# Delta rule's block inverses: the coupling products of both directions, head by head in turn

## The chip, the cores and the metric

The kernel runs on one core of one Trainium2 chip. The metric is the time of one execution on the device, in microseconds (us); the lower, the better. TensorE multiplies matrices, VectorE and ScalarE read its results from PSUM and write them to SBUF, GpSimd does elementwise work from SBUF to SBUF, and the sync engine issues most of the loads.

## The reference

The model is a two-layer backbone over 512 latent tokens and 256 context tokens, 1024 features wide, with feed-forward blocks and adaptive norms around one mixer in each layer. The first layer's mixer has neighbourhood attention beside a gated delta rule, which runs over the tokens in both directions, with four heads of 128 features. Per chunk of tokens and head the delta rule solves a triangular system:

```python
kb = k * beta[..., None]
L = jnp.where(strict, jnp.einsum('bnhcd,bnhsd->bnhcs', kb, k) * decay, 0.0)
A = L + jnp.eye(C, dtype=jnp.float32)
rhs = jnp.concatenate([v * beta[..., None], kb * jnp.exp(g)[..., None]], -1)
sol = lax.linalg.triangular_solve(A, rhs, left_side=True, lower=True, unit_diagonal=True)
u, w = sol[..., :dv], sol[..., dv:]
```

After that a scan over the chunks carries the state S:

```python
v_new = u_i - jnp.einsum('bhcd,bhde->bhce', w_i, S)
o = jnp.einsum('bhcd,bhde->bhce', q_i, S) + jnp.einsum('bhcs,bhse->bhce', qk_i, v_new)
S = S * gl[..., None, None] + jnp.einsum('bhcd,bhce->bhde', k_i, v_new)
```

All arithmetic is float32. Context tokens come first in each direction, and the state they leave starts the latent tokens.

## The kernel before, in words

The whole model is one program for one core, written out engine by engine. `schedule()` makes one list of items, each a piece of TensorE work with its place in PSUM. Every engine walks this list in the same order and picks its share of each item. TensorE executes its queue in list order; at the end of an item it raises the semaphore `product_done` by one, so that a reader of item i waits for `product_done` to reach i + 1. `place` gives each item its PSUM banks, and `before` the earlier items whose banks it takes over: TensorE waits until these have been read (`released`).

The dense products (line 1823) multiply weights and activations that are split into a high and a low part, three matmuls for each product. They fill most of the time.

The delta rule runs in six steps of 128 tokens for each direction. A step has 128 x 128 matrices for four heads and two directions, in tiles [128, 4, 128], one for each direction. For the triangular systems the inverse of A is built by doubling, in `LEVELS` - 1 = 6 levels, k = 1 to 6. A level has three kinds of items, each first for direction 0 and then for direction 1 (`both`):

- N (`dnN`, L1982): the coupling, the product of A's transpose with the inverse so far (X). At k = 1 all of it is multiplied (L1980). From k = 2 on only a quadrant is, 64 output rows of 64 columns for each head: the weights are 64 columns of A's transpose, over all 128 rows of the array, and the moving operand 64 columns of X. `odd_part` says which rows it goes to: partitions 64 to 127 for direction 0, 0 to 63 for direction 1. These are the upper and the lower half of the array's columns. The two directions write to different banks (0 and 2).
- Y (`dnY`, L1997; at k = 6 L1995 with 64 x 64 quadrants): N times Y so far, the transposed inverse of the next level. ScalarE copies it from PSUM (L1245, L1247).
- X (`dnX`, L2004): Y's transpose. VectorE copies the half that is needed (L1693). Level 6 has none.

VectorE reads N between the two (L1684; at k = 6 L1689), with a sign and a rearrangement. A float32 matmul is two instructions in the trace, and so is its weight load; a float32 transpose is one. A direction's N is thus eight instructions of line 1982, and a level has sixteen.

`step()` (line 151) writes down the order: N, Y and X of a level, each for both directions. Into the gaps it puts work of the previous step (`LAST_STEP_AT`: `dnU` at L2027 and `dnO` at L2038, behind N and Y of level 1, X of level 1 and X of level 2) and of the next step (`NEXT_STEP_AT`: `dnA`, products at L1958, behind X of level 3 and Y of level 4; `dnT`, products and transposes, at L1963 and L1967, behind Y of level 5 and N of level 6). Step 0 has no previous step and step 5 no next one, so their gaps lack that work.

For N of k from 2 on, TensorE waits for `x_ready`, the semaphore that VectorE raises with each copy of X, for the direction's own copy, and at k = 2 for ScalarE's rearranged copies of A's transpose too (`at_ready`):

```python
else:
    pe.wait_ge(x_ready, no["dnX"][("dnX", x[1], d, k - 1)] + 1)
if k == 2:
    pe.wait_ge(at_ready, 2 * n + 2)
```

VectorE's side work within a level is in `beside_levels` (line 1525), behind direction 1's items. The state and output updates of the previous step are there (L1498 to L1523) and the next step's masks and products (L1484, L1489, L1545).

The functions that the diff touches:

Of the kernel before, what the change touches and what calls it, by code (L numbers as in the profile page):

```python
# [135 lines left out]
def last_of_group(u):  # L136
    return u % (4 if u < 24 else 2) == (3 if u < 24 else 1)
# [67 lines left out]
def build(nc, a, out, items):  # L205
# [14 lines left out]
    no = {kind: {x: i for i, x in enumerate([x for x in items if x[0] == kind])} for kind in {x[0] for x in items}}  # L220
# [27 lines left out]
    with ExitStack() as ctx:  # L248
# [3 lines left out]
        def sem(name):  # L252
            return ctx.enter_context(nc.semaphore(name))
# [91 lines left out]
        dE, dEM, dEQ, dA, dAT, dQS = ([wb(f"{n}{i}", [P, 4, P]) for i in range(4)] for n in ("dE", "dEM", "dEQ", "dA", "dAT", "dQS"))  # L345
        guard.close()

        dX, dY, dN, dQK = dEM, dE, dA, dEQ
# [36 lines left out]
        product_done = sem("product_done")  # L385
# [34 lines left out]
        def work(x):  # L420

            return 2 * (x[1] % 2) + x[2]

        def group(x):

            return 2 * x[1] + x[2]
# [71 lines left out]
        for x in items:  # L498
            banks = range(place[x][0], sum(place[x]))
            before[x] = list(dict.fromkeys(tenants[b] for b in banks if b in tenants))  # L500
            if x[0] == "O":
# [5 lines left out]
                x = next(("O", u) for u in range(x[1], 56) if last_of_group(u))  # L507
            tenants.update({b: x for b in banks})

        def banks_of(x):  # L510
            return psum[:, 512 * place[x][0]:512 * sum(place[x])]
# [4 lines left out]
        def shift_bank():  # L516
            return psum[:, 512 * 5:512 * 5 + 2]
# [36 lines left out]
        def u_cols(lo, hi):  # L554

            off = U_LAT if hi <= T_LAT else U_CTX - T_LAT
            return slice(lo + off, hi + off)
# [135 lines left out]
        odd_part, even_part = [above, below], [below, above]  # L693
# [12 lines left out]
        def a_odd(x, hd):  # L706

            d, k = x[2], x[3]
            if k == LEVELS - 1:
                return dAT[work(x)][:, hd, odd_part[d]]  # L710
            t = dAT2[d] if k < 4 else dAT4[d]
            return t[:, hd, odd_part[d]] if k % 2 == 0 else t[:, hd, :].rearrange("p (r b) -> p r b", b=2)[:, :, 1 - d]

        def quarter(x):
            return banks_of(x)[:, 0:4 * HALF].rearrange("p (h s) -> p h s", s=HALF)

        def pair4(pair, half):
            return pair[:, 512 * half:512 * half + 512].rearrange("p (h s) -> p h s", s=P)
# [1096 lines left out]
        def _(pe):  # L1815
# [36 lines left out]
            for x in items:  # L1852
                i = number[x]
                pair = banks_of(x)
# [3 lines left out]
                if x == ("start",):  # L1858
                    start_scale(0)
                    pe.wait_ge(start_loaded[0], 16)  # L1860
                    for q in range(KD):
                        ins = nc.tensor.matmul(shift_bank(), ada_start[0][:, P * q:P * q + P], c_cols[:, q, :],
                                               start=q == 0, stop=q == KD - 1)
                    ins.then_inc(shift_product_done, 1)
                    start_scale(1)
                    for k in range(KD):
                        pe.wait_ge(late_lo, k + 1)
                        pe.wait_ge(shift_lo, k + 1)
                        for y in fused:
                            if k == 0:  # L1870
                                pe.wait_ge(lo_split, slot_of[y] + 1)
                            ins = dense_step(y, k, uh, ul)
# [8 lines left out]
                elif x[0] == "norm":  # L1881
# [3 lines left out]
                    if x == final:  # L1885
# [4 lines left out]
                        for t in range(T_LAT // P):  # L1890
                            ins = nc.tensor.matmul(pair[:, 512 * t:512 * t + 1], sq[(KD - 1) % 2][:, P * t:P * t + P], mean_w[:, 0:1],
                                                   start=False, stop=True)
# [3 lines left out]
                    for lo, hi in segs_of(x):  # L1896
                        ins = nc.tensor.matmul(pair[:, lo:hi], mean_w[:, :], sumsq[:, lo:hi], start=True, stop=True)
                    ins.then_inc(product_done, 1)
                elif x[0] == "spread":
                    pe.wait_ge(rstd_ready, len(norm_items))  # L1900
                    for t in range(T_LAT // P):
                        ins = nc.tensor.transpose(pair[:, P * t:P * t + P], rstd[:, t:t + 1].to_broadcast([P, P]), ident[:, :])
                    ins.then_inc(product_done, 1)
                    for t in range(T_LAT // P):
                        ins = nc.tensor.transpose(pair[:, 512 + P * t:512 + P * t + P], rstd[:, t:t + 1].to_broadcast([P, P]), ident[:, :])
                    ins.then_inc(spread_again, 1)
                elif x[0] == "abt":
                    pe.wait_ge(ab_biased, 1)
                    t_ab = out_tile(("proj", 0, "ab", 0))
                    for t in range(STEPS):  # L1910
                        ins = nc.tensor.transpose(pair[:, 16 * t:16 * t + 16], t_ab[0:16, u_cols(P * t, P * t + P)], ident[0:16, 0:16])
# [16 lines left out]
                elif x[0] == "l2":  # L1928
                    j = no["l2"][x]
                    pe.wait_ge(l2_squared, j + 1)  # L1930
                    for lo, hi in (LAT, CTX):
                        ins = nc.tensor.matmul(pair[:, lo:hi], ones_w[:, :], l2_sq[j % 2][:, lo:hi], start=True, stop=True)
                    ins.then_inc(product_done, 1)
                elif x[0] == "cum":
# [4 lines left out]
                    for d in range(2):  # L1939
                        nc.tensor.matmul(cols(0)[:, :, 4 * d:4 * d + 4], masks[:, U[d], :], decay[:, :, 4 * d:4 * d + 4],  # L1940
                                         start=True, stop=True)
                    nc.tensor.matmul(pair[:, 48:96], ones_w[:, :], decay[:, :, :].rearrange("p t c -> p (t c)"),
                                     start=True, stop=True).then_inc(product_done, 1)
# [4 lines left out]
                elif x[0] == "dnA":  # L1948
                    d, tile, b = x[2], SCAN[x[2]][x[1]], work(x)
# [3 lines left out]
                    for hd in range(0 if x[1] else 4):  # L1953
                        c = 4 * d + hd
                        nc.tensor.matmul(pair4(pair, 0)[:, hd, :], decay[:, tile, c:c + 1].to_broadcast([P, P]), masks[:, U[d], :],
                                         start=True, stop=True)
                    for hd in range(4):
                        ins = nc.tensor.matmul(pair4(pair, 1)[:, hd, :], kT[:, hd, :], kT[:, hd, :], start=True, stop=True)  # L1958
                    ins.then_inc(product_done, 1)
                elif x[0] == "dnT":  # L1960
                    d, tile, b = x[2], SCAN[x[2]][x[1]], work(x)
# [4 lines left out]
                    for hd in range(4):  # L1966
                        ins = nc.tensor.transpose(pair4(pair, 0)[:, hd, :], dA[b][:, hd, :], ident[:, :])  # L1967
                    ins.then_inc(product_done, 1)
                elif x[0] == "dnN":
                    d, k, n, b = x[2], x[3], group(x), work(x)  # L1970
                    if k == 1:
                        pe.wait_ge(at_ready, 2 * n + 1)
                        pe.wait_ge(x1_ready, n + 1)
                    else:
                        pe.wait_ge(x_ready, no["dnX"][("dnX", x[1], d, k - 1)] + 1)
                    if k == 2:
                        pe.wait_ge(at_ready, 2 * n + 2)
                    for hd in range(4):
                        if k == 1:
                            ins = nc.tensor.matmul(pair4(pair, 0)[:, hd, :], dAT[b][:, hd, :], dX[b][:, hd, :], start=True, stop=True)  # L1980
                        else:
                            ins = nc.tensor.matmul(quarter(x)[odd_part[d], hd, :], a_odd(x, hd), dX[b][:, hd, even_part[d]],  # L1982
                                                   start=True, stop=True)
                    ins.then_inc(product_done, 1)
                elif x[0] == "dnY":
                    d, k, n, b = x[2], x[3], group(x), work(x)
                    pe.wait_ge(n_ready, no["dnN"][("dnN",) + x[1:]] + 1)
# [5 lines left out]
                    for hd in range(4):  # L1993
                        if k == LEVELS - 1:
                            ins = nc.tensor.matmul(quarter(x)[e, hd, :], dN[b][o, hd, e], dY[b][o, hd, o], start=True, stop=True)  # L1995
                        else:
                            ins = nc.tensor.matmul(pair4(pair, 0)[:, hd, :], (dN[b] if k == 1 else dNI[d])[:, hd, :], dY[b][:, hd, :],  # L1997
                                                   start=True, stop=True)
                    ins.then_inc(product_done, 1)
                elif x[0] == "dnX":  # L2000
                    b = work(x)
                    pe.wait_ge(y_ready, no["dnY"][("dnY",) + x[1:]] + 1)
                    for hd in range(4):
                        ins = nc.tensor.transpose(pair4(pair, 0)[:, hd, :], dY[b][:, hd, :], ident[:, :])  # L2004
                    ins.then_inc(product_done, 1)
                elif x[0] == "dnV":
                    tile = SCAN[x[2]][x[1]]
                    for w, half in ((2, 0), (1, 1))[:1 if x[1] == LAST else 2]:
                        for hd in range(4):
                            ins = nc.tensor.transpose(pair4(pair, half)[:, hd, :], dqkv[:, w, hd, P * tile:P * tile + P], ident[:, :])  # L2010
                    ins.then_inc(product_done, 1)
                elif x[0] == "dnK":
                    d, tile, n, b = x[2], SCAN[x[2]][x[1]], group(x), work(x)
                    pe.wait_ge(s_ready, n - 1)
                    for w, half in ((1, 0), (0, 1)):
                        for hd in range(4):
                            ins = nc.tensor.matmul(pair4(pair, half)[:, hd, :], dqkv[:, w, hd, P * tile:P * tile + P],  # L2017
                                                   dS[d][:, hd, :], start=True, stop=True)
                    ins.then_inc(product_done, 1)
                elif x[0] == "dnU":  # L2020
                    d, n, b = x[2], group(x), work(x)
# [4 lines left out]
                    for hd in range(4):  # L2026
                        ins = nc.tensor.matmul(pair4(pair, 0)[:, hd, :], dY[b][:, hd, :], dVb[b][:, hd, :],  # L2027
                                               start=True, stop=True)
                    ins.then_inc(product_done, 1)
                elif x[0] == "dnO":  # L2030
                    d, n, b = x[2], group(x), work(x)
# [4 lines left out]
                    for lhs, half in ((dQK, 0), (dKd, 1))[:1 if x[1] == LAST else 2]:  # L2036
                        for hd in range(4):
                            ins = nc.tensor.matmul(pair4(pair, half)[:, hd, :], lhs[b][:, hd, :], dVn[b][:, hd, :],  # L2038
                                                   start=True, stop=True)
                    ins.then_inc(product_done, 1)  # L2040
                elif x[0] == "dny":
                    pe.wait_ge(o_normed, DNY.index(x[1]) + 1)
                    for hd in range(4):
                        ins = nc.tensor.transpose(pair4(pair, 0)[:, hd, :], o_acc[:, x[1], P * hd:P * hd + P], ident[:, :])
                    ins.then_inc(product_done, 1)
                elif x[0] == "vt":
                    if x[1] == 0:
                        pe.wait_ge(nv_loaded, 16 * 4)
                        for m in range(2 * x[2], min(2 * x[2] + 2, V_TILES)):
                            first = 64 * m if m < 7 else T_LAT + P * (m - 7)  # L2050
                            for f in range(4):
                                ins = nc.tensor.transpose(pair[:, 512 * (m % 2) + P * f:512 * (m % 2) + P * f + P],
                                                          nv[:, f, first:first + P], ident[:, :])
                    else:
                        pe.wait_ge(odd_read, odd_no[("proj", 1, "v", 1)] + 1)
                        for t in range(3):
                            for f in range(2):
                                m = 3 * x[2] + t
                                ins = nc.tensor.transpose(pair[:, 256 * t + P * f:256 * t + P * f + P],
                                                          sw_v[:, f, P * m:P * m + P], ident[:, :])  # L2060
# [7 lines left out]
                elif x[0] == "S":  # L2068
# [6 lines left out]
                    for part in range(len(heads[0][1])):  # L2075
                        for a_ in range(2):
                            col, n, k = heads[a_][1][part]
                            ins = nc.tensor.matmul(scores(x, a_)[:, col:col + n], heads[a_][0], k, start=True, stop=True)  # L2078
                    ins.then_inc(product_done, 1)
                elif x[0] == "PT":  # L2080
                    u, n = x[1], width(x[1]) // P
                    for a_, normed_by in ((0, p0_normed), (1, p1_normed)):
                        pe.wait_ge(normed_by, u + 1)
                        for c in range(n):
                            ins = nc.tensor.transpose(pair[:, P * (n * a_ + c):P * (n * a_ + c + 1)],  # L2085
                                                      prob(u, a_)[:, P * c:P * c + P], ident[:, :])
# [3 lines left out]
                elif x[0] == "O":  # L2090
# [5 lines left out]
                    n = len(values[0])  # L2096
                    for c in range(n):
                        for a_ in range(2):
                            ins = nc.tensor.matmul(out_bank(x)[HD * a_:HD * a_ + HD, :], values[a_][c], probT(u)[:, n * a_ + c, :],  # L2099
                                                   start=c == 0, stop=c == n - 1)  # L2100
# [120 lines left out]
```

## Time and profile before

| | |
|---|---|
| median of 3 runs | 3043.62 us (3038.5 to 3046.66) |
| profiled execution | 3043.7 us |
| its span, first to last instruction | 3041.9 us |
| TensorE matmuls busy | 2970.7 us, 98% |
| VectorE, ScalarE, GpSimd busy | 1578.4, 946.6, 999.6 us |
| line 1982, all forms | 480 instructions, 31.65 us with at least one in flight |

A row of the timeline is a run of like instructions on one engine: its start from the span's start, the time from the first one's start to the last one's end, engine, line, operation, tiles and shapes, and how many; in brackets the idle time of the engine just before, and what ended it. PE is TensorE's matmuls, PEld its weight loads, DVE VectorE, ACT ScalarE. Matmuls are pipelined: the next one starts before the last has ended, so the time of one is longer than the distance between two. Such a row can hold both directions' instructions, and any wait between them.

### The profile page before, as it was taken

What the parts mean: (1) busy time and instruction counts of PE and PEld (TensorE: products, weight loads), DVE (VectorE), ACT (ScalarE), POOL (GpSimd) and SP (SyncE); (2) the same over time, 40 slices, a digit from 0 to 9 for tenths busy, and PEclk for the clock granted to TensorE, in tenths of its full rate; (3) what the DMA queues carried; (4) which work ended last, traced back from release to release, by engine and by line L of the source; (5) the groups of instructions that cost most, each with busy time, mean ns of one, the idle gap of its engine ahead of it and who ended that gap; (6) DMA issues with size and microseconds to landing.
All of it is one profiled execution on the core that took longest, in us unless ns stands there. A gap on an engine that the chain in (4) does not pass through costs nothing.

```text
span 3041.9 us, 45790 instructions
## 1 busy us (share of the span) xinstructions
PE 2970.7 (98%) x19007; PEld 2784.2 (92%) x19007; DVE 1578.4 (52%) x2456; ACT 946.6 (31%) x1629; POOL 999.6 (33%) x557
## 2 busy tenths in 40 slices
PE   8999999999999988999999999999999999999998
PEld 8999999899888876999999999999999878798997
DVE  7556666884646665567667683212123357421222
ACT  4212212353454455321121232212122236522222
POOL 1333333323332213333333333222222234444443
PEclk9999999999999999999999999999999999999999
DMA  6334444223310022233434431211211210232222
GB/s 251 119 120 136 124 141 141 91 76 125 109 63 8 18 85 76 91 132 132 139 113 144 136 107 63 70 56 61 68 60 56 75 49 2 70 98 93 89 96 70
DMA packets 126379, 285.29 MB, mean 94 GB/s; under 512 B 40238, under 2 KB 57566, under 8 KB 126046
## 3 DMA queue, kind: packets, MB, share of 16 engines
q1 hardware_dynamic: 123438, 275.97, 28.2%
q10 hardware_dynamic: 2736, 6.40, 0.5%
q8 instruction: 151, 2.47, 0.3%
q14 instruction: 54, 0.44, 0.0%
HBM read 270.73 MB, written 15.10 MB: 94 GB/s over the span
## 4 chain that ended last, share of the span: by engine, by line
PE 93%; DVE 3%; ACT 2%; issue 1%; DMA 0%; SPq 0%; POOL 0%; ACTq 0%; POOLq 0%
PE psum L1823 79%; PE psum L1997 2%; PE psum L2099 2%; PE psum L2078 2%; PE psum L2085 2%; DVE o_acc L1647 1%; PE psum L1982 1%; PE psum L2038 1%; PE psum L2017 1%; PE psum L2004 1%; PE psum L1845 0%; PE psum L1963 0%; PE psum L1980 0%; PE psum L1958 0%; PE psum L2027 0%
## 5 line engine op out<-in xcount | busy, mean ns | idle before, releaser
L917 POOL TENSOR_TENSOR wl<-raw,wh 128x1024 fp32r<-128x1024 f32 (+1 forms) x326 | 832.1, 2552 | 1688.4 <-ACT wh L1007 1687.3
L1823 PE MATMUL psum<-uh,wh 128*128 128x256 f32 (+5 forms) x2704 | 661.4, 326 | 7.6 <-POOL wl L917 4.1
L1823 PE MATMUL psum<-uh,wl 128*128 128x256 f32 (+5 forms) x2704 | 657.0, 324 | 0.0
L1823 PE MATMUL psum<-ul,wh 128*128 128x256 f32 (+5 forms) x2704 | 656.9, 324 | 0.0
L1823 PE MATMUL psum<-ah,wh 128*128 128x386 f32 (+4 forms) x2192 | 596.2, 344 | 6.0 <-POOL wl L917 4.7
L1823 PE MATMUL psum<-ah,wl 128*128 128x386 f32 (+4 forms) x2192 | 591.3, 342 | 0.0
L1823 PE MATMUL psum<-al,wh 128*128 128x386 f32 (+4 forms) x2192 | 589.3, 341 | 0.0
L1562 DVE SCALAR_TENSOR_TENSOR ada_product<-ada_w,cb 128x1024 f32<-128x1024 f32 x256 | 478.4, 1869 | 5.1
L1823 PEld LDWEIGHTS psum<-uh,wh 128*128 128x128 f32 (+1 forms) x2704 | 450.9, 189 | 30.8 <-issue 8.8
L1823 PEld LDWEIGHTS psum<-ul,wh 128*128 128x128 f32 (+1 forms) x2704 | 451.3, 189 | 19.2
L1823 PEld LDWEIGHTS psum<-uh,wl 128*128 128x128 f32 (+1 forms) x2704 | 448.8, 189 | 19.9
L1007 ACT ACTIVATE wh<-raw 128x1024 fp32r<-128x1024 f32 (+1 forms) x329 | 336.5, 1025 | 390.1 <-PE psum L1823 377.4
L1823 PEld LDWEIGHTS psum<-ah,wh 128*128 128x128 f32 x2192 | 389.7, 189 | 28.7 <-issue 10.4
L1823 PEld LDWEIGHTS psum<-al,wh 128*128 128x128 f32 x2192 | 389.3, 189 | 17.8
L1823 PEld LDWEIGHTS psum<-ah,wl 128*128 128x128 f32 x2192 | 387.9, 189 | 18.1
L1785 DVE SCALAR_TENSOR_TENSOR h<-psum,mod,h 128x512 f32<-128x512 f32 x192 | 115.3, 635 | 361.8 <-PE psum L1823 361.8
L1385 DVE TENSOR_TENSOR af<-psum,rstd 128x770 f32<-128x770 f32 x66 | 63.3, 959 | 342.7 <-PE psum L1823 342.7
L1092 ACT ACTIVATE sg<-sg 128x512 f32<-128x512 f32 (+1 forms) x154 | 90.4, 628 | 461.0 <-DVE sg L1385 384.0
L1101 ACT ACTIVATE uh<-af 128x768 fp32r<-128x768 f32 x44 | 37.3, 847 | 314.7 <-DVE af L1397 314.7
L1385 DVE TENSOR_TENSOR sg<-psum,rstd 128x770 f32<-128x770 f32 x66 | 63.2, 957 | 116.3 <-PE psum L1823 116.2
L1397 DVE SCALAR_TENSOR_TENSOR af<-af,sg 128x512 f32<-128x512 f32 (+1 forms) x154 | 94.4, 649 | 4.2 <-ACT sg L1092 1.2
L1422 DVE SCALAR_TENSOR_TENSOR cacc<-sq,conv_w,cacc 128x254 f32<-128x254 f32 (+1 forms) x96 | 79.9, 873 | 1.3
(259 smaller groups left out, 2386.4 us busy)
## 6 DMA issues: line engine op xcount, KB each, us to landing
raw<-in_w SPq DMA_DIRECT2D x264, 512.0 KB, 3.7
ada_w<-in_ada_w SPq DMA_DIRECT2D x128, 512.0 KB, 3.7
raw<-in_w SPq DMA_DIRECT2D x64, 448.0 KB, 3.5
spill<-cacc ACTq DMA_DIRECT2D x16, 384.0 KB, 2.5
scale_w<-in_scale_w SPq DMA_DIRECT2D x8, 512.0 KB, 14.6
ada_w<-bias_final SPq DMA_DIRECT2D x16, 256.0 KB, 3.0
ada_start<-in_ada_w SPq DMA_DIRECT2D x7, 512.0 KB, 15.8
h<-in_xT SPq DMA_DIRECT2D x8, 384.0 KB, 15.3
```

The lines of the kernel that those rows point to most:

```text
L917: nc.gpsimd.tensor_tensor(wl[n % SPLIT_SLOTS][:, 0:k * w], raw[n % RAW_SLOTS][:, 0:k * w], wh[n % SPLIT_SLOTS][:, 0:k * w].bitcast(f32), A ...
L1007: nc.scalar.activation(wh[n % SPLIT_SLOTS][:, 0:k * w], raw[n % RAW_SLOTS][:, 0:k * w], ACT.Copy).then_inc(hi_split, 1)
L1092: ins = nc.scalar.activation(t, t, ACT.Silu, bias=b)
L1385: nc.vector.tensor_tensor(t[:, :], bank[:, AT:AT + TU], rstd[rows_, :], ALU.mult).then_inc(scaled, 1)
L1397: ins = nc.vector.scalar_tensor_tensor(out=t, in0=t, scalar=b, in1=sg_part, op0=ALU.add, op1=ALU.mult)
L1422: ins = nc.vector.scalar_tensor_tensor(out=acc, in0=t[:, first + sh - lo:last + sh - lo], scalar=conv_w[:, c, j:j + 1], in1=acc, op0=ALU.m ...
L1562: nc.vector.scalar_tensor_tensor(out=product[:, :], in0=w[:, :], scalar=1.0, in1=cb[:, v, :], op0=ALU.mult, op1=ALU.mult, accum_out=mod[:, ...
L1785: ins = nc.vector.scalar_tensor_tensor(out=h[:, k, lo:hi], in0=banks_of(x)[:, lo:hi], scalar=mod[:, x[1], gate_term(x), k, v:v + 1], in1=h ...
L1823: ins = nc.tensor.matmul(pair[0:w, lo:hi], wt[n % SPLIT_SLOTS][:, k * w:(k + 1) * w], xt[:, k, cols], start=first, stop=last)
L1997: ins = nc.tensor.matmul(pair4(pair, 0)[:, hd, :], (dN[b] if k == 1 else dNI[d])[:, hd, :], dY[b][:, hd, :], start=True, stop=True)
L2078: ins = nc.tensor.matmul(scores(x, a_)[:, col:col + n], heads[a_][0], k, start=True, stop=True)
L2085: ins = nc.tensor.transpose(pair[:, P * (n * a_ + c):P * (n * a_ + c + 1)], prob(u, a_)[:, P * c:P * c + P], ident[:, :])
```

## The change

From k = 2 on, TensorE does nothing at direction 0's N but wait for its banks. At direction 1's N it waits for both directions' copies of X (and at k = 2 both directions' copies of A's transpose) and then issues both products: for each head first direction 0's matmul, then direction 1's. `product_done` is raised with the last head's matmul of each direction, in the same order as before. The readers, the banks, the operands and all other items stay.

```diff
-                elif x[0] == "dnN":
-                    d, k, n, b = x[2], x[3], group(x), work(x)
-                    if k == 1:
-                        pe.wait_ge(at_ready, 2 * n + 1)
-                        pe.wait_ge(x1_ready, n + 1)
-                    else:
-                        pe.wait_ge(x_ready, no["dnX"][("dnX", x[1], d, k - 1)] + 1)
-                    if k == 2:
-                        pe.wait_ge(at_ready, 2 * n + 2)
+                elif x[0] == "dnN" and x[3] == 1:
+                    d, n, b = x[2], group(x), work(x)
+                    pe.wait_ge(at_ready, 2 * n + 1)
+                    pe.wait_ge(x1_ready, n + 1)
                     for hd in range(4):
-                        if k == 1:
-                            ins = nc.tensor.matmul(pair4(pair, 0)[:, hd, :], dAT[b][:, hd, :], dX[b][:, hd, :], start=True, stop=True)
-                        else:
-                            ins = nc.tensor.matmul(quarter(x)[odd_part[d], hd, :], a_odd(x, hd), dX[b][:, hd, even_part[d]],
+                        ins = nc.tensor.matmul(pair4(pair, 0)[:, hd, :], dAT[b][:, hd, :], dX[b][:, hd, :], start=True, stop=True)
+                    ins.then_inc(product_done, 1)
+                elif x[0] == "dnN" and x[2] == 1:
+                    both = [("dnN", x[1], d, x[3]) for d in range(2)]
+                    for y in both:
+                        pe.wait_ge(x_ready, no["dnX"][("dnX", x[1], y[2], x[3] - 1)] + 1)
+                        if x[3] == 2:
+                            pe.wait_ge(at_ready, 2 * group(y) + 2)
+                    for hd in range(4):
+                        for y in both:
+                            ins = nc.tensor.matmul(quarter(y)[odd_part[y[2]], hd, :], a_odd(y, hd), dX[work(y)][:, hd, even_part[y[2]]],
                                                    start=True, stop=True)
-                    ins.then_inc(product_done, 1)
+                            if hd == 3:
+                                ins.then_inc(product_done, 1)
```

## Rows read from the trace of the kernel before

**Rows 1.** The page: busy us (share) xinstructions; the chain's shares by engine and line.
```profile
PE 2970.7 (98%) x19007; PEld 2784.2 (92%) x19007; DVE 1578.4 (52%) x2456; ACT 946.6 (31%) x1629; POOL 999.6 (33%) x557
...
PE 93%; DVE 3%; ACT 2%; issue 1%; DMA 0%; SPq 0%; POOL 0%; ACTq 0%; POOLq 0%
PE psum L1823 79%; PE psum L1997 2%; PE psum L2099 2%; PE psum L2078 2%; PE psum L2085 2%; DVE o_acc L1647 1%; PE psum L1982 1%; PE psum L2038 1%; PE psum L2017 1%; PE psum L2004 1%; PE psum L1845 0%; PE psum L1963 0%; PE psum L1980 0%; PE psum L1958 0%; PE psum L2027 0%
```

**Rows 2.** Windows, 866 to 1093: length, busy PE, PEld, DVE, ACT, POOL; clock; DMA.
```profile
866.00:1093.00 227.00, 209.91 (x2030) 195.33 (x2029) 133.86 (x302) 96.39 (x197) 51.38 (x41) 1.00 0.11 33
```

**Rows 3.** Waits of PE, 866 to 1093: us in total, times, longest.
```profile
PE psum L1997 <- DVE raw L1684: 7.1, 21, 1.1
PE psum L2004 <- ACT dE L1245: 4.0, 15, 0.3
...
PE psum L1982 <- DVE dEM L1693: 2.5, 10, 0.3
```

**Rows 4.** Timeline, step 1, k = 3.
```profile
910.26 0.42 DVE L1693 COPY dEM<-psum 128x256 f32<-128x256 f32 x1 [0.47 <-PE psum L2004]
...
911.94 0.99 PE L1982 MATMUL psum<-dEM,raw 128*64 128x64 f32 x16
912.67 0.88 DVE L1684 TENSOR_TENSOR raw<-psum,couple 64x256 f32<-64x256 f32 x2 [1.99 <-PE psum L1982]
...
913.24 2.02 PE L1997 MATMUL psum<-dE,raw 128*128 128x128 f32 x16 [0.32 <-DVE raw L1684]
```

**Rows 5.** Windows, line 1982: length, busy PE (instructions in flight), PEld; clock; DMA.
```profile
911.90:912.20 0.30, 0.26 (x4) 0.26 (x5) 1.00 0.00 0
...
912.25:912.35 0.10, 0.10 (x7) 0.10 (x7) 1.00 0.00 0
```

**Rows 6.** Timeline, an attention output at line 2099.
```profile
1163.04 1.09 PE L2099 MATMUL psum<-probT_e,v_tile 128*64 128x128 f32 x16 [0.36 <-DVE probT_e L1763]
```

**Rows 7.** Timeline, step 0, k = 2.
```profile
870.16 1.28 PE L1982 MATMUL psum<-dEM,raw 128*64 128x64 f32 x16
870.27 0.42 DVE L1693 COPY dEM<-psum 128x256 f32<-128x256 f32 x1 [0.53 <-PE psum L2004]
```

**Rows 8.** Timeline, step 1, k = 5.
```profile
922.18 0.86 DVE L1693 COPY dEM<-psum 128x256 f32<-128x256 f32 x2 [0.74 <-PE psum L2004]
...
922.75 1.10 PE L1982 MATMUL psum<-dEM,raw 128*64 128x64 f32 x16 [0.17 <-DVE dEM L1693]
923.45 0.88 DVE L1684 TENSOR_TENSOR raw<-psum,couple 64x256 f32<-64x256 f32 x2 [0.41 <-PE psum L1982]
...
924.02 0.46 PE L1997 MATMUL psum<-dE,raw 128*128 128x128 f32 x2 [0.17 <-DVE raw L1684]
```

**Rows 9.** Timeline, step 1, k = 6.
```profile
928.02 0.75 DVE L1693 COPY dEM<-psum 128x256 f32<-128x256 f32 x2
...
928.58 0.98 PE L1982 MATMUL psum<-dEM,dAT 128*64 128x64 f32 x16 [0.33 <-DVE dEM L1693]
929.27 0.88 DVE L1689 TENSOR_SCALAR dA<-psum 64x256 f32<-64x256 f32 x2 [0.50 <-PE psum L1982]
...
929.49 1.16 PE L1963 MATMUL psum<-dqkv 128*128 128x128 f32 x8
...
931.02 0.96 PE L1995 MATMUL psum<-dE,dA 64*64 64x64 f32 x16
```

**Rows 10.** Timeline, step 5, k = 4 and k = 6.
```profile
1079.91 1.33 PE L1982 MATMUL psum<-dEM,raw 128*64 128x64 f32 x16
1081.08 0.69 DVE L1523 TENSOR_TENSOR o_acc<-psum,o_acc 128x512 f32<-128x512 f32 x1
...
1091.11 0.43 DVE L1689 TENSOR_SCALAR dA<-psum 64x256 f32<-64x256 f32 x1 [0.18 <-PE psum L1982]
1091.76 0.42 DVE L1689 TENSOR_SCALAR dA<-psum 64x256 f32<-64x256 f32 x1 [0.22 <-PE psum L1982]
```

## The prediction

> **What bounds the kernel now.** Start with the page's busy table and chain [rows 1]: TensorE is busy 98% of the span, and the chain that ended last runs through it for 93%, so a delay in TensorE's queue moves the end unless a later wait swallows it. Most of that chain is line 1823, the dense products, which the change doesn't touch; line 1982, the matmuls it reorders, is 1%. Next the stretch of the six scan steps [rows 2]: the block inverses lie between 866 and 1093 us, and the granted clock there is 1.00, the 2.4 GHz level, so the clock is no term of the sum. Then the waits of TensorE in that stretch [rows 3]: before Y it waits for VectorE's read of the coupling product N (line 1684), 7.1 us, before X for ScalarE, 4.0 us, and before N for VectorE's copy of X, 2.5 us. Last the timeline of single levels, by which the sum below goes.
>
> A level is a loop through three engines: N (L1982), VectorE's read of N (L1684, at k = 6 L1689), Y (L1997, at k = 6 L1995), ScalarE's copy, X (L2004), VectorE's copy of X (L1693), the next N. In [rows 4], the level k = 3 of step 1, N starts at 911.94, VectorE reads direction 0's product from 912.67, and Y starts at 913.24, while VectorE is still at direction 1's product (two reads of 0.44 in the row of 0.88). So Y starts when direction 0's product has been read. Direction 1's is read second, directly behind the first, and its Y stands on TensorE behind eight instructions of 0.11 us.
>
> **The change part by part.** Nothing is computed more or less: there are 30 levels (k = 2 to 6 in six steps), each with 16 instructions of line 1982, eight of a direction. Two things move. Direction 0's eight now stand behind direction 1's wait for its copy of X; and the two directions alternate.
>
> *What alternating gives.* In [rows 5] four instructions are in flight in the first 0.3 us of the level at 911.94, and seven in the 0.1 us from 912.25 on: direction 1's already run beside direction 0's last ones, and the 16 take 0.99 us [rows 4]. That the two column halves can run side by side throughout is shown by line 2099, which alternates halves: 16 instructions with 128 moving columns take 1.09 us [rows 6], where 16 of line 1997, on all 128 columns with as many moving, take 2.02 [rows 4]. So I take full overlap, and with it 0.68 us for the 16, an estimate: from N's start to VectorE's first read pass 0.73 us in rows 4, less some 0.05 for the signal, which is what direction 0's eight need alone (0.058 each from start to start, and the rest for the last to end). Direction 0 then ends as long after its start as before, direction 1 some 0.31 earlier (0.99 - 0.68). That is worth nothing by itself: VectorE reads direction 0's product first, and direction 1's was there when it was free.
>
> The Trainium skill's page "TensorE: Matmul & The Clock Gate", section "What overlaps and what doesn't", says that a weight load runs beside matmuls in flight only if it is for another row group, and that matmuls start and end strictly in order. Both directions use all 128 rows, so by that rule the halves wouldn't overlap; line 2099's rows speak against it. What it would do here is the first rival.
>
> *What the joined wait costs.* It depends on whether both copies of X are there when TensorE reaches N. From a copy's end to N's start I read 0.14 us: in [rows 8] the two copies take 0.86 from 922.18, so the first ends at 922.61, and N starts at 922.75. After the change N starts 0.14 after the second copy. The 30 levels are of five kinds:
>
> 1. Other work stands between X and N on TensorE (the next step's lines 1958 or the last step's 2038): k = 2, 3, 4 of steps 1 to 4, k = 4 of step 0, k = 2 and 3 of step 5, 15 levels. In [rows 4] direction 1's copy ends at 910.68, and N starts at 911.94. Cost 0.
> 2. k = 5 of steps 0 to 4, 5 levels [rows 8]: the second copy ends at 923.04, N could start at 923.18 in place of 922.75. Y follows directly on the read of direction 0's product (from 923.45, Y at 924.02): 0.43 each, 2.15 in all.
> 3. k = 6 of steps 0 to 4, 5 levels [rows 9]: the copies end at 928.77, N starts at 928.91, 0.33 later. But between N and Y stand 12 instructions of the next step, from 929.49 until Y at 931.02, and they cover the read at 929.27. What counts is when N's last instruction leaves TensorE: before, 0.98 after 928.58, 929.56; then 928.91 + 0.68 = 929.59. Cost 0.03 each, 0.15 in all; without that cover 0.33 each.
> 4. No other work, and the two transposes of X apart: k = 2 and 3 of step 0 and k = 5 of step 5, 3 levels, the first shown [rows 7]. N starts at 870.16 before direction 1's copy, which ends at 870.69; the new start is 870.83. Cost 0.67 each, 2.01 in all.
> 5. As kind 4, with something else behind, in step 5 [rows 10]. At k = 4 N starts at 1079.91, but VectorE is at line 1523 until 1081.77; direction 0's product, ready at 1080.59 and with 0.67 more at 1081.26, waits for that anyway. Cost 0. At k = 6 the small Y of direction 1 follows on its own read. That began at 1091.76; it now stands behind the first read, which moves from 1091.11 to 1091.78 and takes 0.43, so it begins at 1092.24: cost 0.48.
>
> Sum: 0 + 2.15 + 0.15 + 2.01 + 0 + 0.48 = 4.8 us. Behind the waiting instructions on TensorE stand only this level's Y and, at k = 6, the next step's products; both are in the sum. VectorE's and ScalarE's side work between levels comes as much later as TensorE does. The changed lines issue no DMA.
>
> Two costs no row shows. The alternating order: from -0.31 us a level (if direction 1's earlier end counted, in the 15 levels of kind 1) to +0.35 (no overlap: direction 0's last instruction is the 14th in the row and no longer the eighth, 6 x 0.058); I take 0, since line 2099, the nearest row, shows full overlap. The joined wait: from 0 (all swallowed later) to 6.5 (2.15 + 2.01 + 5 x 0.33 without cover + 0.67 at the last level); I take 4.8.
>
> The profiled execution took 3043.7 us (span 3041.9 and 1.8 around it), as good as the median of the three runs, 3043.62. Forecast: 3043.7 + 4.8 = 3048.5 us, 0.16% more. Under 0.3%, some 9 us, a measurement of this kernel can't tell it from no change.
>
> **The rivals.**
>
> *The halves don't overlap when they take turns* (where the page's rule would lead). Place: N in every level. Direction 0's product is complete 0.35 us later in the 15 levels of kind 1, the 5 of kind 2, the 3 of kind 4 and the last level: 24 x 0.35 = 8.4. At k = 6 of steps 0 to 4 the 16 take 0.93 + 0.22 = 1.15 in place of 0.68: 5 x 0.47 = 2.35. With 4.8 that is 15.5: 3059 us, slower by 0.5%. It decides from 0.18 us a level on (24 x 0.18 = 4.3, which with 4.8 makes 9.1). For it: TensorE now changes halves with every matmul. Against: rows 5 and 6.
>
> *The delays are swallowed*: 3044 to 3046 us. For: TensorE waits for other engines elsewhere in the step, 4.0 us before X alone [rows 3]. Against: what it waits for there follows on TensorE's own earlier work, and comes later with it.
>
> *Direction 1's earlier end reaches the path*: 15 x 0.31 = 4.65 back for 4.8 paid, 3044 us. For: N holds TensorE for 0.31 us less. Against: TensorE idles 0.32 us before Y in rows 4 as it is.
>
> **How the numbers follow.** Forecast 0.72, no overlap 0.10, swallowed 0.13, path shortened 0.05. The three runs lie between 3038.5 and 3046.7, so I put some 3 us of scatter below the lowest case, 3044, and end the range just under the highest: 3041 to 3058. Slower by over 0.3%: nearly all of the first rival, 0.09, and scatter above the forecast, 0.05, together 0.14. Faster by over 0.3%: no case has it; 0.02 for scatter. The rest, 0.84, is within 0.3%.
>
> **What the profile after would show.** Right: N's 16 instructions in some 0.68 us in every level, with no wait inside; VectorE's two reads of N back to back everywhere; N 0.14 after the second copy of X at k = 5 of steps 0 to 4 and in kind 4, and Y as much later. Wrong: N over 0.9 us in its row (first rival), Y starting sooner after X than now in a level of kind 1, or the stretch of the six steps as long as before.

## The result, and the profile after

The changed kernel takes 3047.64 us (median of 20 runs, 3043.7 to 3052.56) against 3040.95 for the kernel before in the same runs: ratio 1.0022, 95% interval 1.0016 to 1.0029, so 6.7 us slower by the medians. Forecast were 3048.5 us, which is 4.8 us more than the 3043.7 that the forecast started from.

The changed kernel's page has the same picture as [rows 1]: TensorE first, in the busy table and in the chain.

```profile
PE 2963.3 (97%) x19007; PEld 2776.3 (91%) x19007; DVE 1578.4 (52%) x2456; ACT 946.4 (31%) x1629; POOL 998.6 (33%) x557
...
PE 92%; DVE 3%; ACT 2%; issue 1%; DMA 0%; POOL 0%; SPq 0%; ACTq 0%; POOLq 0%
```

Its waits of TensorE between 860 and 1100 us (in total, times, longest) are where the loss shows. Before Y they have grown from the 7.1 us of [rows 3] to 14.5, before N from 2.5 to 9.5. The first is no loss: N takes TensorE less long, and the time it gives back is spent waiting for the same read. The second is the joined wait.

```profile
PE psum L2000 <- DVE raw L1684: 14.5, 23, 1.1
PE psum L1984 <- DVE dEM L1693: 9.5, 15, 0.7
PE psum L2007 <- ACT dE L1245: 4.0, 15, 0.3
```

(N is line 1984 now, Y 2000, at k = 6 1998, X 2007.) Three levels of step 1 in the changed kernel's timeline, k = 3, 5 and 6, answer to [rows 4, 8 and 9] (a row's count can be cut short by the end of the window that was asked for; Y has 16 instructions in each level):

```profile
915.03 0.42 DVE L1693 COPY dEM<-psum 128x256 f32<-128x256 f32 x1 [0.47 <-PE psum L2007]
...
916.71 0.70 PE L1984 MATMUL psum<-dEM,raw 128*64 128x64 f32 x16
917.44 0.88 DVE L1684 TENSOR_TENSOR raw<-psum,couple 64x256 f32<-64x256 f32 x2 [1.99 <-PE psum L1984]
918.01 0.46 PE L2000 MATMUL psum<-dE,raw 128*128 128x128 f32 x2 [0.61 <-DVE raw L1684]
...
926.94 0.86 DVE L1693 COPY dEM<-psum 128x256 f32<-128x256 f32 x2 [0.74 <-PE psum L2007]
927.95 0.70 PE L1984 MATMUL psum<-dEM,raw 128*64 128x64 f32 x16 [0.61 <-DVE dEM L1693]
928.66 0.88 DVE L1684 TENSOR_TENSOR raw<-psum,couple 64x256 f32<-64x256 f32 x2 [0.85 <-PE psum L1984]
929.23 1.02 PE L2000 MATMUL psum<-dE,raw 128*128 128x128 f32 x7 [0.58 <-DVE raw L1684]
...
933.23 0.74 DVE L1693 COPY dEM<-psum 128x256 f32<-128x256 f32 x2
...
934.12 0.69 PE L1984 MATMUL psum<-dEM,dAT 128*64 128x64 f32 x16 [0.67 <-DVE dEM L1693]
934.74 1.16 PE L1963 MATMUL psum<-dqkv 128*128 128x128 f32 x8
...
936.26 0.85 PE L1998 MATMUL psum<-dE,dA 64*64 64x64 f32 x14
```

At k = 3 N's 16 instructions have shrunk from 0.99 us to 0.70, but from the copy of X to Y pass 918.01 - 915.03 = 2.98 us, to the hundredth what they took before (913.24 - 910.26). TensorE idles 0.61 before Y and no longer 0.32: all that N gained is waited away. At k = 5 the same distance is 2.29, before 1.84: 0.45 lost. At k = 6 it is 3.03, before 3.00.

In the first trace of the changed kernel one thing more stands in the stretch that the prediction's sum doesn't have. In step 0 the granted clock falls to its lower level, 1.2 GHz, for a little over 3 us, in which Y's 16 instructions take 3.57 us and not 2.02. The windows (length; busy PE, PEld, DVE, ACT, POOL; clock; DMA) and the row:

```profile
866.00:873.00 7.00, 4.90 (x48) 4.22 (x48) 2.82 (x5) 3.41 (x5) 1.81 (x2) 1.00 0.40 150
873.00:877.00 4.00, 3.52 (x17) 3.55 (x18) 2.00 (x4) 0.60 (x1) 0.00 (x0) 0.59 0.24 80
```

```profile
873.48 3.57 PE L2000 MATMUL psum<-dE,raw 128*128 128x128 f32 x16 [0.53 <-issue]
```

### The profile page after: what moved, and what is told of

The parts are those of the page before. It is cut to its first block, busy times and chain, and to the rows that moved or that the text cites. A ratio compares the mean times of both kernels' runs of the same rounds, so it can differ in the third digit from the quotient of the medians.

```text
span 3050.8 us, 45796 instructions
## 1 busy us (share of the span) xinstructions
PE 2963.3 (97%) x19007; PEld 2776.3 (91%) x19007; DVE 1578.4 (52%) x2456; ACT 946.4 (31%) x1629; POOL 998.6 (33%) x557
## 4 chain that ended last, share of the span: by engine, by line
PE 92%; DVE 3%; ACT 2%; issue 1%; DMA 0%; POOL 0%; SPq 0%; ACTq 0%; POOLq 0%
PE psum L1823 79%; PE psum L2000 2%; PE psum L2102 2%; PE psum L2088 2%; PE psum L2081 2%; DVE o_acc L1647 1%; PE psum L2041 1%; PE psum L1984 1%; PE psum L2020 1%; PE psum L2007 1%; PE psum L1845 0%; PE psum L2030 0%; ACT cacc L1132 0%; PE psum L1974 0%; PE psum L1963 0%
```

## The experiments

The theory is that the joined wait costs what it delays direction 0 wherever no other work covers it, and that the turns themselves cost nothing, and give something only where TensorE has other instructions directly behind N, as at k = 6 of steps 0 to 4. Its rivals: the turns cost; or the clock does.

To compare traces without the scatter elsewhere, take the stretch from the first X in step 0 (the second level of the inverse begins behind it) to the transposes of v behind the last level of step 5, on TensorE's timeline. In the kernel before:

```profile
868.66 0.61 PE L2004 MATMUL psum<-ident,dE 128*128 128x128 f32 x4
...
1092.90 1.09 PE L2010 MATMUL psum<-ident,dqkv 128*128 128x128 f32 x8
```

which is 224.24 us. Each ratio in the table is against the kernel before in the same runs (its medians there: 3040.95 in the first runs, 3041.32 in those of the joined wait, of the turns where covered and of one split, 3040.61 in the others).

| kernel | stretch, us | against 224.24 | median us | ratio to before, interval |
|---|---|---|---|---|
| before, second trace | 224.27 | 0.0 | (one run) | |
| changed, four traces | 230.74, 230.67, 230.36, 229.15 | +6.5, +6.4, +6.1, +4.9 | 3047.64; again 3046.88 | 1.0022; again 1.0018 (1.0009 to 1.0027) |
| joined wait, no turns, two traces | 230.44, 230.43 | +6.2 | 3047.65 | 1.0021 (1.0012 to 1.0029) |
| turns only where covered | 224.26 | 0.0 | 3040.44 | 0.9995 (0.9986 to 1.0004) |
| turns only where not covered | 230.33 | +6.1 | 3049.36 | 1.0023 (1.0013 to 1.0032) |
| one split, no turns | 220.63 | -3.6 | 3041.38 | 0.9997 (0.9988 to 1.0005) |
| one split, turns | 217.81 | -6.4 | 3034.74 | 0.998 (0.9971 to 0.9989) |
| two splits, no turns | 217.78 | -6.5 | 3034.64 | 0.9977 (0.9969 to 0.9986) |
| two splits, turns | 214.06 | -10.2 | 3032.23 | 0.997 (0.9959 to 0.9981) |

**The joined wait without the turns.**

```diff
-                    for hd in range(4):
-                        for y in both:
+                    for y in both:
+                        for hd in range(4):
```

> The changed kernel, but with direction 0's four matmuls first and then direction 1's: the joined wait without the turns. Joined wait as the cause: as slow as the changed kernel or slightly slower, +5.5 to +7.5 us over the kernel before (2.2 at k = 5 of steps 0 to 4, 2.0 in three levels of kind 4, 0.5 at the last level, and 0.33 in place of 0.03 in the five levels of kind 3, as the 16 instructions take 0.97 us again). Turns as the cause: within 1 us of the kernel before.

As slow as the changed kernel: 3047.65 us, and the stretch 6.2 longer where 6.4 were expected of the wait. At k = 5 of step 1 its timeline shows the same late N (the copies take 0.86 from 924.69 and end at 925.55), though the 16 instructions take 0.96 us:

```profile
924.69 0.86 DVE L1693 COPY dEM<-psum 128x256 f32<-128x256 f32 x2 [0.74 <-PE psum L2007]
...
925.70 0.96 PE L1984 MATMUL psum<-dEM,raw 128*64 128x64 f32 x16 [0.61 <-DVE dEM L1693]
```

The wait alone makes a loss of this size. The turns as its cause have fallen.

They even give some of it back. The changed kernel's one stretch without a fall of the clock (229.15 us, below) is 1.3 us shorter than this one, and the place is k = 6 of steps 0 to 4, as expected. In step 1 of the joined wait without turns:

```profile
930.97 0.74 DVE L1693 COPY dEM<-psum 128x256 f32<-128x256 f32 x2
...
931.86 0.94 PE L1984 MATMUL psum<-dEM,dAT 128*64 128x64 f32 x16 [0.66 <-DVE dEM L1693]
...
932.73 1.16 PE L1963 MATMUL psum<-dqkv 128*128 128x128 f32 x8
...
934.25 0.96 PE L1998 MATMUL psum<-dE,dA 64*64 64x64 f32 x16
```

From the copies to Y pass 934.25 - 930.97 = 3.28 us, against 3.03 with turns and 3.00 in the kernel before. Here the next step's instructions stand directly behind N, and a shorter N lets them start sooner. By the medians the two kernels are equal all the same (3047.64 and 3047.65): in three of the changed kernel's four traces a fall of the clock, below, takes about as much.

**Turns only where both copies are there anyway, and the complement.**

```diff
+                elif x[0] == "dnN" and not in_turn(x):
+                    (as before the change, for one direction)
...
+        def in_turn(x):
+            return (x[3] in (2, 3) and x[1] > 0) or (x[3] == 4 and x[1] < LAST)
```

(The second piece stands further up in the file.) The complement returns the contrary.

> Turns and joined wait only in the 15 levels of kind 1, where both copies of X are there anyway; the order and the waits of the kernel before in the other 15. Joined wait as the cause: within 1 us of the kernel before, N's 16 instructions in 0.69 us at these levels and Y as long after N's start as before. Turns as the cause: about half of the slowdown stays, +3 us or more.

> The complement of the kernel with turns in the covered levels only: turns and joined wait in the other 15 levels (k = 5 and 6 of steps 0 to 4, k = 2 and 3 of step 0, k = 4 to 6 of step 5). Joined wait as the cause: all of the slowdown, +5 to +7 us over the kernel before, and the same shifts level by level as in the changed kernel (0.44 at k = 5, 0.03 at k = 6, 0.68 or a little more at the others). Turns as the cause: half of it, +3 to +3.5.

In the covered half, the stretch is as before to 0.02 us, and the time too (0.9995). In the other half all the loss is there: +6.1, of which a fall of the clock in step 5 is some 1.2 (below). Had the turns been the cause, each half would have had half of it.

**The changed kernel again, for the clock.** The medians' 6.7 us are more than the 4.9 of the trace in which the clock stays up. Is a fall of the clock within the steps the change's?

> The changed kernel once more. Its first trace has the clock at its lower level for 3.4 us during Y at k = 2 of step 0, where the kernel before had it at 861. If that fall comes with the change (TensorE idles longer there): the clock falls within step 0 again, and the stretch of the six steps is 6.5 to 7 us longer than before. If it is chance: it falls elsewhere, as in the other traces at 861, and the stretch is 5.0 to 5.5 us longer, which is the joined wait alone.

> The kernel before, a second trace. In its first one the clock falls once for 3.4 us at 861, before step 0, and not within the six steps. If falls within the steps come with turns in the levels without cover: none within them here either. If they come by chance: one here is as likely as in the changed kernel.

> The changed kernel, a third trace. In both so far the clock falls for 3.4 us within the steps, once in step 0 and once in step 5, which costs some 1.5 us each. If that comes with the change: again a fall in step 0 or step 5 and the stretch 6.4 us or more longer than before. If by chance: none, and 5.0 to 5.5 us longer.

> The changed kernel, a fourth trace, for the same count: with the change a fall in step 0 or step 5, by chance none.

> The joined wait without turns, a second trace. In its first the clock didn't fall within the steps, though the wait is the same: N keeps TensorE busy for 0.97 us there and not for 0.69. If the shorter N with the wait makes the clock fall: none here. If the wait alone does, or chance: one in step 0 or 5 here.

Within the steps the clock falls in three of four traces of the changed kernel (once in step 0, twice in step 5) and in the one with turns only where not covered (step 5). It doesn't in two traces of the kernel before and two of the joined wait without turns. A fall costs 1.2 to 1.6 us, the distance of the first three lengths in the table from the fourth. What TensorE does before it differs a little: in the third trace of the changed kernel it is busy 3.98 of 6.50 us ahead of the fall, in the joined wait without turns 4.53 over the same work, which runs 1.27 us later there (N at k = 3 of step 5 starts at 1080.70 and not at 1079.43).

```profile
1080.00:1086.50 6.50, 3.98 (x46) 3.27 (x40) 5.70 (x14) 1.19 (x2) 0.00 (x0) 1.00 0.01 4
1086.50:1091.00 4.50, 4.44 (x24) 4.12 (x24) 0.79 (x2) 1.19 (x2) 0.00 (x0) 0.62 0.00 0
```

```profile
1081.27:1087.77 6.50, 4.53 (x51) 3.81 (x45) 5.70 (x14) 1.19 (x2) 0.00 (x0) 1.00 0.02 4
```

But in the fourth trace of the changed kernel it is busy as little, and the clock stays up:

```profile
1079.90:1086.40 6.50, 4.01 (x46) 3.29 (x42) 5.68 (x14) 1.20 (x2) 0.00 (x0) 1.00 0.01 4
1086.40:1090.90 4.50, 3.54 (x36) 3.11 (x38) 1.24 (x3) 1.20 (x2) 0.00 (x0) 1.00 0.00 0
```

So the count speaks for falls that come with waits and short N together, but it is four of five against none of four, and what decides in a single run stays open. Nor is it clear that these falls are extra ones. Both traces of the kernel before have a fall of 3.4 us just ahead of the steps (granted clock 0.72 from 860 to 866); in the first and the third trace of the changed kernel and in the one with turns only where not covered it is missing there (1.00), while the second has both. The second trace of the joined wait has neither, so a missing fall ahead of the steps doesn't by itself bring one within them.

Nor is the rest of the program equal from trace to trace. The fourth trace of the changed kernel takes 6.4 us more in all than the first one of the kernel before: 4.9 in the stretch, 0.3 ahead of it and 1.2 behind it, where one spell of the lower clock lasts 13.6 us and not 10.2:

```profile
1188.70:1198.90 10.20, 7.57 (x33) 5.80 (x30) 1.58 (x5) 1.73 (x5) 5.78 (x3) 0.50 0.45 141
```

```profile
1191.80:1205.40 13.60, 9.98 (x46) 7.47 (x47) 2.56 (x8) 3.71 (x8) 8.02 (x6) 0.50 0.31 95
```

(The first is the kernel before, the second that fourth trace.)

**Work behind N.** If the shorter N is waited away before Y, it should count once TensorE has something to do there. Line 2038's product of the last step has an output half and a state half of eight instructions each. The second one goes behind N, as an item of its own (`dnS`), at k = 2 for direction 0 and k = 3 for direction 1:

```diff
-LAST_STEP_AT, NEXT_STEP_AT = (0, 1, 2, 5), (8, 10, 13, 15)
+LAST_STEP_AT, NEXT_STEP_AT = (0, 1, 2, 5, 3, 6), (8, 10, 13, 15)
-            for i, x in zip(LAST_STEP_AT, both("dnU", st - 1) + both("dnO", st - 1)):
+            for i, x in zip(LAST_STEP_AT, both("dnU", st - 1) + both("dnO", st - 1) + both("dnS", st - 1)):
...
-                    for lhs, half in ((dQK, 0), (dKd, 1))[:1 if x[1] == LAST else 2]:
-                        for hd in range(4):
-                            ins = nc.tensor.matmul(pair4(pair, half)[:, hd, :], lhs[b][:, hd, :], dVn[b][:, hd, :],
+                    for hd in range(4):
+                        ins = nc.tensor.matmul(pair4(pair, 0)[:, hd, :], (dQK if x[0] == "dnO" else dKd)[b][:, hd, :], dVn[b][:, hd, :],
...
```

> The kernel before with the last step's product of line 2038 split into its two halves of eight instructions: the output half stays before N at k = 2 (direction 0) and k = 3 (direction 1), the state half goes behind N, into TensorE's idle time before Y. If that idle time is what bounds these levels: 0.42 us less in ten levels (k = 2, 3 of steps 1 to 5), -4.2 us against the kernel before. If other waits take its place: within 1 us.

> The same split, with turns in the 15 levels of kind 1 as in the kernel with turns only there. If the shorter N counts once TensorE has work to go on with: in ten levels 16 instructions leave 0.35 to 0.4 us sooner, so 3 to 4 us less than the split alone, some -8 us against the kernel before. If VectorE's read bounds the level all the same: as the split alone, within 1 us.

First without turns, then with them, k = 3 of step 1 (N, the state half and Y are lines 1984, 2037 and 1999 in the first, 1999, 2053 and 2015 in the second):

```profile
910.73 0.99 PE L1984 MATMUL psum<-dEM,raw 128*64 128x64 f32 x16
911.46 0.88 DVE L1686 TENSOR_TENSOR raw<-psum,couple 64x256 f32<-64x256 f32 x2 [1.09 <-PE psum L1984]
911.64 1.16 PE L2037 MATMUL psum<-dAT,dA 128*128 128x128 f32 x8
912.64 1.95 PE L1999 MATMUL psum<-dE,raw 128*128 128x128 f32 x16
```

```profile
910.93 0.70 PE L1999 MATMUL psum<-dEM,raw 128*64 128x64 f32 x16
...
911.55 1.16 PE L2053 MATMUL psum<-dAT,dA 128*128 128x128 f32 x8
911.66 0.88 DVE L1690 TENSOR_TENSOR raw<-psum,couple 64x256 f32<-64x256 f32 x2 [1.09 <-PE psum L1999]
912.55 1.95 PE L2015 MATMUL psum<-dE,raw 128*128 128x128 f32 x16
```

Y has no idle time in front in either. From N to Y pass 1.91 us without turns and 1.62 with them: the turns are now worth 0.29 a level. Over ten levels the split alone shortens the stretch by 3.6 us, with turns by 6.4; 4.2 and some 8 were expected. The time bears out the second, -6.6 us by the medians. The first it leaves open (0.9997): six of its eleven runs were at a mean granted clock of 0.992 and took 3041.4 to 3042.8 us, the five at 0.994 to 0.996 took 3033.6 to 3037.0. Beside runs of the kernel before at the same mean clock both groups are faster (3043.4 to 3046.7 at 0.992; 3038.8 to 3041.9 at 0.994 to 0.996), which agrees with the stretch.

**Cover for k = 5 and 6.** The next step's products of line 1963 are taken from their transposes (`dnQ`) and put between X and N (in part, against the split with turns):

```diff
-LAST_STEP_AT, NEXT_STEP_AT = (0, 1, 2, 5, 3, 6), (8, 10, 13, 15)
+LAST_STEP_AT, NEXT_STEP_AT = (0, 1, 2, 5, 3, 6), (8, 10, 13, 15, 11, 14)
...
-            return (x[3] in (2, 3) and x[1] > 0) or (x[3] == 4 and x[1] < LAST)
+            return (x[3] in (2, 3) and x[1] > 0) or (x[3] >= 4 and x[1] < LAST)
```

> The split kernel with turns, and the next step's products of line 1963 taken apart from the transposes behind them: direction 0's go between X of k = 4 and N of k = 5, direction 1's between X of k = 5 and N of k = 6, so that these ten levels too have both copies of X when TensorE reaches N; turns there as well. If the joined wait costs nothing once covered, and TensorE's idle time before N bounds k = 5 and 6: 0.8 to 1.2 us less in each of steps 0 to 4, 4 to 6 us below the split with turns, -10 to -12 us against the kernel before. If ScalarE's copies bound the end of a step: 1 us or less below the split with turns.

> The same order of items, but no turns and no joined wait anywhere. If turns are worth 0.29 us a level where TensorE has work behind N: 4 to 6 us slower than the same order with turns (10 levels of k = 2 and 3, 5 of k = 6, a part at k = 5). If they are worth nothing: the same within 1 us.

With turns at the 25 levels that now have cover this is the fastest version: 3032.23 us, ratio 0.997 (0.9959 to 0.9981), faster than both kernels. The stretch is 3.8 us shorter than with one split, a little under the 4 to 6 expected. Without the turns, the same order is 3.7 us longer in the stretch and 2.4 by the medians, also under the 4 to 6 expected; the intervals of these two overlap, so the stretch shows it and the time only points that way. The levels say where the turns pay here: at k = 5 of step 1 TensorE has nothing between N and Y, and from N to Y pass 1.31 us with turns and without; at k = 6, with four transposes in between, 1.29 with and 1.48 without.

## Why the prediction was right

The working of the 4.8 us holds term by term. That the forecast of 3048.5 us comes within 1 us of the 3047.64 measured is in part luck: its starting point, 3043.7 from three runs and the profiled one, is 2.7 us above the median of 20 runs, 3040.95, and the 4.8 us are 1.9 below the 6.7 by the medians; the two errors nearly cancel. The prediction also took anything under 0.3% for lost in the noise; 20 runs of each kernel told 0.22% from no change.

Term by term, from the starts of direction 1's Y in the fourth trace of the changed kernel, in which the clock doesn't fall within the steps, against the kernel before:

| step of the prediction | forecast, us a level | measured |
|---|---|---|
| 1. covered, 15 levels | 0 | 0 to 0.03 |
| 2. k = 5, steps 0 to 4 | 0.43 | 0.44 |
| 3. k = 6, steps 0 to 4 | 0.03 | 0.03 to 0.04 |
| 4. step 0 k = 2, k = 3; step 5 k = 5 | 0.67, 0.67, 0.67 | 0.76, 0.65, 0.65 |
| 5. step 5 k = 4; k = 6 | 0; 0.48 | 0; 0.46 |
| sum | 4.8 | 4.9 |

The one level that is off is k = 2 of step 0: N starts 0.26 us after the second copy of X there (871.59 + 0.42 to 872.27 in the first trace) and not 0.14. At k = 2 TensorE has two more waits in the row, for the rearranged copies of A's transpose, which ScalarE had long finished (by 868.22 in that trace). That going through these waits takes the extra 0.1 us is a guess; no run leaves them out. A slip in the sum: at k = 6 of step 5 the prediction's own 1091.78 + 0.43 is 1092.21 and not 1092.24, so the cost is 0.45 by its numbers; it changes the sum by 0.03.

*The turns.* Full overlap was the chosen end, and N's 16 instructions take 0.69 to 0.70 us in every level, 0.68 forecast, which was an estimate. The rule of the Trainium skill that stood beside the first rival ("TensorE: Matmul & The Clock Gate", "What overlaps and what doesn't") is against this: all 128 rows are in use, and weight loads and matmuls of the two column halves run side by side all the same (the 16 matmuls in 0.70 us, their 16 weight loads within the first 0.56 of it at k = 3 of step 1); the measurement decides. Another page has what became of the gain: "TensorEngine Tiling (Array Packing)", section "PSUM Bottleneck", says that tiling speeds up TensorE but not the reading of PSUM, which may then bind (it says so of a fourfold speedup). The trace agrees, at a smaller one. Here N went from 0.99 to 0.70 us, and the read from 0.88 to 0.88.

*Swallowed, or given back to the path*: neither. The stretch is longer by all that the sum has, and Y starts no sooner in any covered level. The only gain of the turns is the one that the sum counts, 0.03 us lost a level and not 0.28 at k = 6 of steps 0 to 4.

*What the sum lacked.* It held the clock for no term, from the 1.00 of [rows 2]. That was true of the kernel before and of one trace in four of the changed one; in the others a fall within the steps adds 1.2 to 1.6 us to the stretch, which makes it 6.0 us longer on the mean of the four. What else lies between the 4.8 us and the medians' 6.7 isn't shown: the fourth trace has 1.2 us more behind the steps, where the clock is low for longer, and whether the change brings that no run says. The whole-run scatter of 3 us and more, before and after, is of the same kind: in the 33 runs of the kernel before beside the first experiments, those at 0.992 took 3043.4 to 3046.7 us, those at 0.994 to 0.997 3036.7 to 3041.9.

## What to carry to other kernels

Two chains that alternate on one engine hide each other's latency because they are out of step; a joint start makes the first wait for the second, and pays wherever no third work stands in the gap. A shorter step is worth what the next instruction on its engine can do with it: the same turns gave 0 us a level with an idle gap behind them, 0.25 at k = 6 of steps 0 to 4 in the changed kernel, where the next step's instructions stand there, and 0.29 with eight instructions put into the gap. So fill the gap first, from work that can be cut in two, one part ahead of the step and one behind it.

## What was not expected of the hardware

In the kernel before, direction 1's matmuls didn't wait for direction 0's to be through: with both inputs there, [rows 4 and 5] have them run side by side although the queue holds eight instructions of one half and then eight of the other. So part of what turns could give was taken already, 0.99 us for what takes 1.28 with a wait between. And a clock that stands at its upper level in a profile of one kernel is no constant for the next: in three traces of four of the changed kernel it was at half for 3.4 us within steps in which both traces of the kernel before have it at 1.00. That the waiting brings it isn't shown: the joined wait without turns waits as long before N (0.61 us at k = 5) and had no fall there in two traces.
